# Hybrid attention and gMLP layer: a different order of squares, scaling, transposes and projection blocks at the head of the kernel

## The reference

```python
hp = rms_norm(yp, g_mix[l])                 # y * rsqrt(mean(y*y) + 1e-6) * g
q, k, v, u, g = project(hp, w_in[l])        # hp @ w_in, 1024 -> 1792 columns
a = window_attention_prompt(q, k, v, attn_sinks[l])
m = gmlp_prompt(u, g, gmlp_ln_g[l], gmlp_ln_b[l], gmlp_w_spatial[l], gmlp_b_spatial[l])
yp = yp + jnp.concatenate([a, m], axis=-1) @ w_out[l]
...                                         # the same for the 32 sample rows, against a cache
yp = yp + swiglu(rms_norm(yp, g_ffn[l]), w_gate[l], w_up[l], w_down[l])
y_prompt = rms_norm(yp, g_final)
```

## Time and profile before

| What | us |
|---|---|
| median of 3 runs | 1065.97 (1063.82 to 1066.91) |
| the profiled execution, its own time | 1065.66 |
| its span in the profile | 1063.9 |
| PE busy | 1022.2 (96%) |
| DVE busy | 625.9 (59%) |
| ACT busy | 391.0 (37%) |
| POOL busy | 385.3 (36%) |

### The profile page before, as it was taken

The page is one execution under the profiler, slowest core; times in us unless marked ns, Lnnn a source line. Parts: engine busy times, 40 slices in busy tenths (PEclk is TensorE's granted clock), DMA queues, the critical chain, the costliest instruction groups (busy, mean ns, idle before and its releaser), DMA issues.

```text
span 1063.9 us, 19541 instructions
## 1 busy us (share of the span) xinstructions
PE 1022.2 (96%) x7160; PEld 934.2 (88%) x7160; DVE 625.9 (59%) x943; ACT 391.0 (37%) x763; POOL 385.3 (36%) x445
## 2 busy tenths in 40 slices
PE   5999999999999699999999999999999969999996
PEld 5999998888887599999999999999999737877785
DVE  5376547665444766666676576567665554454524
ACT  5412144444232433333333333333334354424331
POOL 2010100000000437676686596686762300120045
PEclk9999999999999899999999999999999989999999
DMA  8211331101222434364454544643637898777714
GB/s 282 90 39 42 81 83 43 40 1 64 95 100 90 116 97 147 109 198 133 124 173 123 159 140 125 186 144 110 188 117 261 271 359 293 240 267 254 269 40 163
DMA packets 176258, 155.84 MB, mean 146 GB/s; under 512 B 22352, under 2 KB 143760, under 8 KB 176208
## 3 DMA queue, kind: packets, MB, share of 16 engines
q1 hardware_dynamic: 176208, 155.16, 46.1%
HBM read 114.17 MB, written 41.06 MB: 146 GB/s over the span
## 4 chain that ended last, share of the span: by engine, by line
PE 88%; DVE 4%; DMA 4%; POOL 1%; issue 1%; ACT 1%; SPq 0%; POOLq 0%; ACTq 0%; DVEq 0%
PE ps L1033 27%; PE ps L1034 26%; PE ps L1035 26%; DMA xd_in<-act_scratch 2%; PE ps L1070 1%; PE ps L1364 1%; PE ps L1205 1%; PE ps L1183 1%; DMA act_scratch<-act_sums 1%; DMA out_state_gmlp_v_sample<-work 1%; PE ps L1167 1%; DVE work L1831 1%; DMA y_acc_odd<-in_w_down 1%; DVE ln_st L1825 1%; DMA gain<-in_g_mix 0%
## 5 line engine op out<-in xcount | busy, mean ns | idle before, releaser
L1033 PE MATMUL ps<-x_forms,w_forms 128*128 128x256 f32 (+1 forms) x1232 | 354.0, 287 | 10.5 <-DVE w_forms L1746 8.3
L1034 PE MATMUL ps<-x_forms,w_forms 128*128 128x256 f32 (+1 forms) x1232 | 355.0, 288 | 0.0
L1035 PE MATMUL ps<-x_forms,w_forms 128*128 128x256 f32 (+1 forms) x1232 | 353.6, 287 | 0.0
L1033 PEld LDWEIGHTS ps<-x_forms,w_forms 128*128 128x128 f32 x1232 | 236.3, 192 | 11.2 <-DVE w_forms L1746 5.8
L1035 PEld LDWEIGHTS ps<-x_forms,w_forms 128*128 128x128 f32 x1232 | 236.1, 192 | 0.0
L1034 PEld LDWEIGHTS ps<-x_forms,w_forms 128*128 128x128 f32 x1232 | 235.8, 191 | 0.0
L1033 PE MATMUL ps<-w_dn,x_dn 128*128 128x512 f32 x308 | 121.3, 394 | 0.0
L1035 PE MATMUL ps<-w_dn,x_dn 128*128 128x512 f32 x308 | 119.9, 389 | 0.0
L1034 PE MATMUL ps<-w_dn,x_dn 128*128 128x512 f32 x308 | 119.9, 389 | 0.0
L1746 DVE TENSOR_TENSOR w_forms<-w_sums,w_forms 128x512 fp32r<-128x512 f32 x88 | 74.1, 843 | 68.1 <-ACT w_forms L1570 67.7
L885 POOL TENSOR_SCALAR meansq<-sumsq 128x1 f32<-128x1 f32 (+1 forms) x27 | 10.4, 386 | 256.3 <-ACT xn_ffn L1410 227.0
(11 more groups left out here) (234 smaller groups left out, 2071.2 us busy)
## 6 DMA issues: line engine op xcount, KB each, us to landing
xd_in<-act_scratch SPq DMA_DIRECT2D x35, 512.0 KB, 7.1
t_raw<-in_w_down SPq DMA_DIRECT2D x88, 128.0 KB, 2.6
act_scratch<-act_sums SPq DMA_DIRECT2D x22, 512.0 KB, 4.0
y_acc_odd<-in_w_down SPq DMA_DIRECT2D x22, 512.0 KB, 5.6
wd_in<-t_scratch SPq DMA_DIRECT2D x20, 512.0 KB, 7.1
wd_in<-in_w_down SPq DMA_DIRECT2D x15, 512.0 KB, 6.2
stage<-in_w_in SPq DMA_DIRECT2D x28, 256.0 KB, 3.6
w_stage_even<-in_w_gate SPq DMA_DIRECT2D x22, 256.0 KB, 3.4
```

Of the source, the lines that this page charges most:

```text
L1033: mm(out, wh, xh, start=first, stop=False, skip_group_check=onto)
L1034: mm(out, wh, xl, start=False, stop=False, skip_group_check=onto)
L1035: return mm(out, wl, xh, start=False, stop=last, skip_group_check=onto)
```

## The change

Four edits, all at the head (and the line numbers move by one):

1. `xn` has four slots in place of two (`XN_SLOTS`), and Sq(r) waits for T(r-4).
2. The first 29 items of `make_schedule` stand in another order. Three fronts come first, then the backs of tiles 0 and 1, split 0, the back of tile 2, the front of tile 3 and split 1. From then on half blocks, backs and fronts alternate. Block 0's first half stands before the back of tile 3. Each front now stands behind the back of the tile just before it, where it stood behind the back of the tile two before.
3. SP loads tile 1 before the gain vector in place of after it.
4. The mask of the spatial matrix comes behind R(8), and POOL's wait for it before R(4) goes.

```diff
+XN_SLOTS = 4
...
-    s = [("front", 0), ("front", 1), ("back", 0), ("front", 2), ("split", 0), ("back", 1),
-         ("front", 3), ("back", 2), ("split", 1), ("front", 4), ("back", 3), ("front", 5),
-         ("block", 0, 0), ("back", 4), ("front", 6), ("block", 0, 1), ("back", 5), ("front", 7),
-         ("evac", 0), ("block", 1, 0), ("back", 6), ("front", 8), ("block", 1, 1), ("back", 7),
-         ("evac", 1), ("block", 2, 0), ("back", 8), ("block", 2, 1), ("evac", 2),
+    s = [("front", 0), ("front", 1), ("front", 2), ("back", 0), ("back", 1), ("split", 0),
+         ("back", 2), ("front", 3), ("split", 1), ("block", 0, 0), ("back", 3), ("front", 4),
+         ("block", 0, 1), ("evac", 0), ("back", 4), ("front", 5), ("block", 1, 0), ("back", 5),
+         ("front", 6), ("block", 1, 1), ("evac", 1), ("back", 6), ("front", 7), ("block", 2, 0),
+         ("back", 7), ("front", 8), ("block", 2, 1), ("evac", 2), ("back", 8),
...
-        xn = work[:, 0:2048].rearrange("p (s c) -> p s c", s=2)
+        xn = work[:, 0:4096].rearrange("p (s c) -> p s c", s=XN_SLOTS)
...
             load_rows(0)
+            load_rows(1)
             sp.dma_start(gain[:, :], a["g_mix"][0].partition_broadcast(P)).then_inc(gain_landed, 16)
-            load_rows(1)
...
-                    if item == ("front", 4):
-                        pool.wait_ge(tril_ready, 1)
                     root(item[1])
-                if item == ("back", 2):
+                if item == ("back", 8):
...
-                    pool.wait_ge(rstd_ready, 4)
+                    pool.wait_ge(rstd_ready, ROWS)
...
-                if 2 <= r < ROWS:
-                    act.wait_ge(turned, r - 1)
+                if XN_SLOTS <= r < ROWS:
+                    act.wait_ge(turned, r - XN_SLOTS + 1)
```

More of the change, by code:

```diff
@@ L1067, in norm_back @@
                 out = turned_pair(r)
-                src = xn[rows, i % 2, :] if r < ROWS else xn_ffn[rows, :]
+                src = xn[rows, i % XN_SLOTS, :] if r < ROWS else xn_ffn[rows, :]
                 for k in range(KT):
@@ L1404, in norm_front @@
                     act.wait_ge(cat_lo, ROWS)
-                if 2 <= r < ROWS:
-                    act.wait_ge(turned, r - 1)
+                if XN_SLOTS <= r < ROWS:
+                    act.wait_ge(turned, r - XN_SLOTS + 1)
                 if ROWS < r < 2 * ROWS:
                     act.wait_ge(turned, r)
-                dst = xn[rows, i % 2, :] if r < ROWS else xn_ffn[rows, :] if r < 2 * ROWS else squares(r)
+                dst = xn[rows, i % XN_SLOTS, :] if r < ROWS else xn_ffn[rows, :] if r < 2 * ROWS else squares(r)
                 nc.scalar.activation(dst, src, ACT.Square,
@@ L1764, in norm_front @@
                 dve.wait_ge(rstd_ready, r + 1)
-                dst = xn[rows, i % 2, :] if r < ROWS else xn_ffn[rows, :] if r < 2 * ROWS else src
+                dst = xn[rows, i % XN_SLOTS, :] if r < ROWS else xn_ffn[rows, :] if r < 2 * ROWS else src
                 nc.vector.scalar_tensor_tensor(out=dst, in0=src, scalar=rstd[rows, r:r + 1],
```

## The result

| | us |
|---|---|
| changed kernel, median of 6 runs | 1080.46 (1079.66 to 1084.21) |
| kernel before, median of 6 runs | 1065.23 (1063.82 to 1066.91) |
| ratio | 1.0151, 95% interval 1.0131 to 1.0170 |
| changed kernel's profiled execution, own time and span | 1083.66 and 1081.9 |

The change makes the kernel 15.2 us slower by the medians; 14.5 were forecast. The profiled execution is one of the two longer runs of the six (1083.66 and 1084.21; the other four lie between 1079.66 and 1080.62), 18.0 us over that of before (1083.66 - 1065.66), so the parts read from it add up to 18 and not to 15.

The account below looks back on a forecast made before the run. PE, busy for 96% of the span, was taken as the bound, so its idle time at the head counts in full. A 12.2 us delay plus 2.3 for the clock gave 14.5 us on 1065.66, so 1080.2, range 1076 to 1085.

Parts of the forecast that it names:

- The front behind the back of the tile before: At the head, a 5.50 us chain against 2.96 of work idles PE 2.54 us before T(4) to T(8): 12.7 us lost.
- The strict order of ScalarE's queue: On ACT, Sq(r+1) cannot overtake the waiting C(r); if it could, none of the 12.7 us would arise.
- The first half block: Block 0 starts at 18.1 in place of 19.34, gaining 1.2 us; bounds 17.5 and 19.3.
- Gain after tile 1: At the start, N(0) moves to near 7.8, costing T(0) 1.3 us, covered by tile 2's load; taken as nothing.
- Mask, splits, evacuations, SP's queue: On POOL, ACT and SP at the head and behind it, these edits and shifts neither gain nor cost: nothing.
- The clock: PE's idle times at the head bring the lower clock in half the turns: 2.3 us, bounds nothing to 6.4.
- The sum: Over the whole kernel, 12.2 us at full clock plus 2.3 for the clock: 14.5 us slower, 1080.2.
- A later wait taking it back: Rival: PE's later waits for FFN and down-projection, 19.6 us together, swallow the delay; 1065.3, chance 0.04.
- The work ahead holding: Rival: fronts run ahead through the four slots, PE stays dense, only the start counts: -0.4 us, 1065.3, chance 0.03.
- The clock high all the time: Rival: PE's clock stays high through the idle times, leaving 12.2 us: 1077.9, chance 0.20.
- Low all the time: Rival: PE's clock stays low from block 0 to T(8), 12.2 + 6.4 = 18.6 us: 1084.3, chance 0.13.

Follow-up runs that it names:

- ahead: The changed kernel with fronts 4 to 8 each one item earlier, so two tiles ahead; 1066.97 us, 1.0008 of the kernel before.
- behind: The kernel before with only fronts 4 to 8 moved behind the back of the tile just before; 1080.70 us, ratio 1.0134.
- again: The changed kernel itself, unaltered, measured once more; 1082.48 us, 1.0151 of the kernel before.
- gain_first: The changed kernel with the gain vector loaded ahead of tile 1 again; 1080.92 us, 1.0143 of the kernel before.
- loads_mask: The kernel before with only tile 1 loaded ahead of the gain vector and the mask behind R(8); 1066.85 us, ratio 1.0010.
- warm: The kernel before with extra unread matmuls in PE's idle times ahead of T(0) to T(3); 1063.46 us, ratio 0.9975.
- fill: The changed kernel with seven extra unread matmuls on PE ahead of each of T(4) to T(8); 1080.74 us, 1.0141 of the kernel before.
- fill_again: The changed kernel with seven extra unread matmuls ahead of each of T(4) to T(8), measured a second time; 1078.99 us, 1.0123 of the kernel before.
- once: The changed kernel with fronts 4 and 5 behind back 3 and later fronts two tiles ahead; 1071.72 us, 1.0044 of the kernel before.

## Why the prediction was right

- *The front behind the back of the tile before, 12.7 us.* Right in place, kind and size. The chain is 5.50 to 5.55 us where the transpose is short, as worked out. The five gaps sum to 11.0 us (2.37 + 2.36 + 1.63 + 2.34 + 2.30): each a little under 2.54, and the third short because the half block ahead of it ran at the lower clock. That the place of the fronts is the cause is shown both ways, by ahead (taken out, the loss goes) and by behind (put alone into the kernel before, it comes).
- *The strict order of ScalarE's queue.* The prediction left open whether a ready instruction can pass a waiting one. The trace of after shows it cannot here: Sq(4) had its rows at 16.9 and its slot free, and waited behind C(3) until 25.90, with ACT idle for 5.28 us ahead of C(3). The Trainium skill, "TensorE: Matmul & The Clock Gate", section "Architectural detail: the array is 16× 32×32, not 1× 128×128", says that ScalarE takes its queue in strict order, and these 5.28 us agree. VectorE's order was not put to the test.
- *The first half block at 18.1, a gain of 1.2 us.* Too good by 1.0: it started at 19.13. The square of tile 2 began at 10.01, not 9.2, as that load landed later than in the trace of before; the rest of the chain added the other 0.2. In the profile of again it began at 17.49, so this term moves by more than a microsecond between executions. T(2) lasted 1.07 there and 1.94 here. With the later start and the long turns T(8) stood at 52.43, a little beyond the 50 to 52 that the prediction named.
- *Gain after tile 1, at nothing.* Right: gain_first starts N(0) 2.05 us earlier and block 0 at the same place. The cost was underrated for N(0) itself (8.64, not 7.8), and without its cover it is about 1 us (loads_mask).
- *Mask, splits, evacuations, SP's queue, at nothing.* Right as far as the runs tell: ahead, which has them all, is level with before, and its "consts" follow T(8) by the same work as there (54.20 - 38.76 = 15.4 us; before 52.67 - 35.13 less the half block of 2.1, which is 15.4 too).
- *The clock, 2.3 us of 0 to 6.4.* Right in sign and within its bounds; the size was too small for the profiled execution. There it is 4.6 (0.8 and 0.9 for the two long turns, 2.9 behind T(8)), and the profile of again shows the same turns (29.3 us from T(3) to T(8)) and the same 2.9 behind. The prediction counted the turns and, in the likeliest case, nothing behind T(8); of the whole 18.0 us in the profiled execution this is what lies over the forecast, beside block 0.
- *The sum, 14.5 us.* The medians differ by 15.2, the profiled executions by 18.0. That the forecast is within 1 us of the medians is in part luck: on the profiled execution, for which it was worked out, block 0 was put 1.0 too early and the clock's part 2.3 too small. The eleven runs of the change lie in two groups, six from 1079.66 to 1080.62 and five from 1082.48 to 1084.21, and both profiles were taken from the upper one. The 2.9 us behind T(8) would be of the size that parts them, but no profile of a run of the lower group was taken, so this is not shown.
- *The rivals.* A later wait taking it back: wrong, the waits around 370 and 830 are as long as before (19.8 against 19.6 us). The work ahead holding: wrong. The clock high all the time: only with fillers. Low all the time: not seen, long and short transposes alternate.

## What to carry to other kernels

More slots don't give a lead; the list gives it. Where one list orders all engines, count the chain from one use of the bottleneck engine to the next that hangs on it, and compare it with the work that this engine has in between: here 5.5 us against 2.96 with one tile of lead and 5.92 with two. A gap on PE costs more than its length, as the clock may fall behind it; and where idle time at the start can't be avoided, harmless matmuls in it can be worth more than another order: here warm is at 0.9975 and ahead at 1.0008.

## What the runs showed of the hardware that I had not expected

Transposes alone can raise PE's clock, by their durations. The Trainium skill says that the full clock does not engage for transposes ("TensorE: Matmul & The Clock Gate", section "Part 4: PE-mode transpose"), and the trace of before seemed to agree, with T(0) to T(3) at 1.97 each. But in again PE had run nothing but T(0) and T(1), back to back, when T(2) lasted 1.07:

```profile
9.10 3.68 PE L1069 MATMUL ps<-ident,work 128*128 128x128 f32 x16 [9.10 <-DVE work L1765]
13.84 1.07 PE L1069 MATMUL ps<-ident,work 128*128 128x128 f32 x8 [1.07 <-DVE h_first L1745]
17.49 0.66 PE L1032 MATMUL ps<-h_first,wbuf 128*128 128x384 f32 x1 [2.58 <-DVE h_first L1745]
```

The measurement decides. T(2) lasted 1.07 in fill and fill_again too, which have no fillers that early, and 1.94 in the profiles of the changed kernel, ahead and once, with the same instructions of PE up to there. After the gap of 2.58 us block 0 ran at the lower level once more, by the granted clock of its first 3.5 us (columns as in the earlier trace rows):

```profile
17.50:21.00 3.50, 3.50 (x11) 0.50 0.84 271
```

So the same work meets the clock differently from one execution to the next. That may be one reason why the changed kernel's runs spread over 4.5 us and those of before over 3.1; it is not shown.
